# Attention scores of a hybrid decoder layer as split products over 128 rows, with a third weight place for one more unit

## Chip, cores, metric

One NeuronCore of a Trainium2 chip runs the whole layer. The metric is the device time of one execution in microseconds (us), the median over several executions; lower is better. Engines are named as in the profile: PE is TensorE (PEld its weight loads), DVE VectorE, ACT ScalarE, POOL GpSimd, SP SyncE, which here only issues DMAs.

## What is computed

One decoder layer over 512 tokens of width 1024, in float32. One input projection gives the inputs of two token mixers and their gates. Mixer A is a gated linear recurrence (4 heads of 128). Mixer B, which the change touches, scores all causal keys with a small indexer, keeps the 128 best keys of each query, and attends to these with 8 heads of 64 and a T5 relative bias. Cut to what matters:

```python
proj = einsum('bld,dn->bln', x, w_in) + b_in
score = einsum('bth,bths->bts', w, relu(q_idx . k_idx))    # indexer, 8 heads of 64
idx = top_k(where(causal, score, -inf), 128)               # per query, shared by heads
logits = q . k[idx] * 64 ** -0.5 + rel_bias[t5_bucket(qpos - idx)]
ob = softmax(logits) . v[idx]
merged = sigmoid(ga) * ((norm(oa) * silu(za)) @ w_up_a) + sigmoid(gb) * ((ob * silu(zb)) @ w_up_b)
out = layer_norm(ALPHA * x + merged @ w_out)
```

## The kernel before

**Split products.** float32 accuracy of the large projections comes from splitting both operands into a high part in float32r (fp32r, reduced float32) and a low part, the rest. `split_product` (lines 478 to 481) then issues three products: high x high, high x low, low x high. ScalarE makes the high parts of the weights (`split_hi`, line 792), GpSimd or VectorE the low parts (`split_lo`, lines 1570 and 1399).

**Units and quarters.** The weight matrix is cut into units of 256 columns (`UNITS`; the index is the unit's number: 7 is qb0, 8 kb0, 9 and 10 vb, 11 qb1, 12 kb1, 13 and 14 ia, 15 and 16 fa, 17 and 18 qa, 19 to 22 ga). A unit is four quarters of twelve products with 512 columns, and the quarter q is the clock of everything: each engine runs its own hand-written loop over q and calls `side(q)`, which holds the work that is planned beside the projections. On TensorE `side(q)` comes behind quarter q's products, in order; nothing is reordered at run time, and the engines meet at semaphores alone. A unit's first half fills `proj_bank[0]`, its second half `proj_bank[1]`. Each must be emptied (`leave_bank`, line 812 on ScalarE and 1140 on VectorE) before the next unit's same half, two quarters after it was filled. For qb and kb, ScalarE empties it with one activation and the bias (line 859); for vb and ia it is VectorE with an addition (line 1167).

**Weights.** SyncE loads a unit's raw weights, 1 MB in two halves, into one of two raw places by parity; the load of unit u waits for the low parts of unit u-2 (`wait_lo`). High and low parts have three places (`SLOTS`, `slot`): the third is shared in time with x, with gate inputs and with the residual. `hi_quarter(u)` is the quarter in which ScalarE rounds unit u: 4(u-1), or earlier for units in `EARLY_HI`. VectorE makes the low parts of units 17 to 24 (`LO_DVE`), piece 0 in the quarter behind that, pieces 1 to 3 one later (`low_parts`).

**Mixer B.** The indexer's products `dots` (lines 600 and 601) run in quarters 12 to 23, two heads a quarter, as fp32r over 128 rows: the query tile holds a head's high and low part one above the other. VectorE sums them into `score[b]` for query blocks b = 1, 2, 3 with (b+1) x 128 keys. Then `topk_round` (lines 1206 and 1207), 16 rounds per block that each find and strike out 8 keys, following `topk_rounds()`; a last pass makes the penalty tile `pen[b]`. Attention is 32 items (b, head), in pairs, first heads 0 to 3, then 4 to 7; `Q_ITEM` says in which quarter. For an item: `scores` on TensorE (line 611, one fp32 product over the head's 64 rows; the heads of a pair lie in rows 0 to 63 and 64 to 127), GpSimd prepares bias plus penalty in `logit`, `logits` on VectorE subtracts and takes the maximum (line 1230), `softmax_exp` on ScalarE, `invert_sums` on VectorE (line 1241), `normalise` on ScalarE, two quarters later `turn_probs` (transposes, line 620), `move_probs` on VectorE, and `attend` (line 635). The order within VectorE's `side(q)` is: leave bank, index scores, moves, gates, logits, top-k rounds, reciprocals, low parts, mixer A.

**Mixer A.** `tree` holds its products by level (64, 32, ... 1), for p = 0 from quarter 73 and p = 1 from 82 (`Q_TREE`). ScalarE computes the exponentials of each level (`level_factors`) behind VectorE's distances (line 424) and copies results of levels 64 and 32 out of the banks (`tree_copy`, lines 959 and 967); the banks `log_bank` are two, taken in turn.

## Time and profile before

| What | Value |
|---|---|
| median of 3 runs | 469.42 us (469.35 to 471.55) |
| the profiled execution | 468.56 us, of it span 466.8 us |
| TensorE / its weight loads | 456.4 us (98%) / 362.9 us (78%) |
| VectorE, ScalarE, GpSimd busy | 281.4, 217.7, 162.4 us |
| mean granted TensorE clock | 0.995 of 2.4 GHz |
| DMA | 45.64 MB, mean 98 GB/s |

Read it as: the execution's own time holds the span, from its first to its last instruction, and 1.8 us around it. Busy times of engines overlap. TensorE's products are pipelined, so a product's own duration is longer than the step from its start to the next one's; the steps are what adds up.

### The profile page before, as it was taken

How to read it: one execution, taken by the hardware profiler on the slowest of the kernel's cores; microseconds unless marked ns; L12 is line 12 of the kernel's file. 1: busy time of each engine (PE TensorE's matmuls, PEld its weight loads, DVE VectorE, ACT ScalarE, POOL GpSimd, SP SyncE). 2: the span in 40 equal slices, each digit the busy share in tenths (PEclk: the TensorE clock that was granted, in tenths of full speed). 3: DMA queues.
4: the chain of work that ended last, by engine and by line, in shares of the span. 5: the costliest groups of instructions: out<-in, count | busy, mean ns of one | idle time of the engine just before them, and what ended most of it. 6: DMA issues, size and time to landing. Idle time of an engine off the chain costs nothing.

```text
span 466.8 us, 7633 instructions
## 1 busy us (share of the span) xinstructions
PE 456.4 (98%) x2970; PEld 362.9 (78%) x2970; DVE 281.4 (60%) x542; ACT 217.7 (47%) x369; POOL 162.4 (35%) x161
## 2 busy tenths in 40 slices
PE   8999999999999999999999899999999999999993
PEld 6778888888777777777887687787888888888883
DVE  4446589999995333343999984971532332562286
ACT  5635454341327445274876666825872333341000
POOL 0444442492259823481004000000044444994000
PEclk9999999999999999999999999999999999999997
DMA  8818112243022420202021220222033232275022
GB/s 269 268 44 292 57 68 91 90 163 108 0 91 67 134 72 1 91 0 92 18 95 70 91 93 2 93 93 90 0 120 136 87 110 90 94 242 207 0 90 91
DMA packets 15876, 45.64 MB, mean 98 GB/s; under 512 B 2232, under 2 KB 3808, under 8 KB 15840
## 3 DMA queue, kind: packets, MB, share of 16 engines
q1 hardware_dynamic: 15600, 44.96, 28.7%
q8 instruction: 24, 0.39, 0.3%
q10 hardware_dynamic: 240, 0.20, 0.1%
q14 instruction: 12, 0.10, 0.1%
HBM read 43.04 MB, written 2.11 MB: 97 GB/s over the span
## 4 chain that ended last, share of the span: by engine, by line
PE 89%; DVE 6%; issue 2%; ACT 1%; DMA 1%; DVEq 0%; SPq 0%; ACTq 0%
PE bank L479 25%; PE bank L481 24%; PE bank L480 24%; PE bank L611 3%; PE bank L707 2%; PE bank L682 2%; PE bank L635 2%; PE bank L620 2%; DVE w_lo L1399 1%; DMA w_raw<-in_w_units 1%; PE bank L601 1%; PE bank L600 1%; PE bank L525 1%; PE bank L521 1%; PE bank L693 1%
## 5 line engine op out<-in xcount | busy, mean ns | idle before, releaser
L1570 POOL TENSOR_TENSOR w_lo<-w_raw,w_hi 128x512 fp32r<-128x512 f32 x92 | 120.9, 1344 | 166.9 <-ACT w_hi L792 160.2
L479 PE MATMUL bank<-x_hi,w_hi 128*128 128x512 f32 x336 | 134.6, 400 | 0.0
L481 PE MATMUL bank<-x_hi,w_lo 128*128 128x512 f32 x336 | 131.1, 390 | 0.0
L480 PE MATMUL bank<-x_lo,w_hi 128*128 128x512 f32 x336 | 131.0, 390 | 0.0
L479 PEld LDWEIGHTS bank<-x_hi,w_hi 128*128 128x128 f32 x336 | 63.0, 188 | 18.1 <-issue 5.5
L481 PEld LDWEIGHTS bank<-x_hi,w_lo 128*128 128x128 f32 x336 | 63.1, 188 | 13.7
L480 PEld LDWEIGHTS bank<-x_lo,w_hi 128*128 128x128 f32 x336 | 63.2, 188 | 12.0
L792 ACT ACTIVATE w_hi<-w_raw 128x1024 fp32r<-128x1024 f32 (+1 forms) x66 | 66.7, 1028 | 10.9 <-PE bank L481 5.5
L877 ACT ACTIVATE prob<-prob,nmax 128x128 f32<-128x128 f32 (+3 forms) x32 | 17.8, 556 | 47.5 <-DVE nmax L1230 47.4
L1218 DVE COPY prob_t<-bank 128x128 f32<-128x128 f32 (+3 forms) x32 | 14.2, 485 | 31.7 <-PE bank L620 31.6
L1206 DVE MAX8 best<-score 128x8 f32<-128x256 f32 (+2 forms) x48 | 26.8, 558 | 1.0
L1207 DVE MATCH_REPLACE8 score<-best,score 128x256 f32<-128x256 f32 (+2 forms) x48 | 26.0, 542 | 0.0
L479 PE MATMUL bank<-w_hi,x_hi 128*128 128x512 f32 x64 | 25.8, 403 | 0.0
L1399 DVE TENSOR_TENSOR w_lo<-w_raw,w_hi 128x512 fp32r<-128x512 f32 x36 | 23.4, 686 | 3.4 <-ACT w_hi L792 3.4
L481 PE MATMUL bank<-w_hi,x_lo 128*128 128x512 f32 x64 | 25.0, 391 | 0.0
L480 PE MATMUL bank<-w_lo,x_hi 128*128 128x512 f32 x64 | 24.9, 390 | 0.0
L479 PE MATMUL bank<-o_hi,w_hi 128*128 128x512 f32 x64 | 24.9, 389 | 0.0
L480 PE MATMUL bank<-o_lo,w_hi 128*128 128x512 f32 x64 | 24.9, 389 | 0.0
L481 PE MATMUL bank<-o_hi,w_lo 128*128 128x512 f32 x64 | 24.9, 389 | 0.0
L1588 POOL TENSOR_TENSOR logit<-t,pen 128x256 f32<-128x256 f32 x24 | 17.4, 742 | 11.9 <-DVE nmax L1230 11.9
L885 ACT ACTIVATE prob<-prob,prob_rcp 128x128 f32<-128x128 f32 (+3 forms) x32 | 16.3, 556 | 10.3 <-DVE prob_rcp L1241 10.3
L1196 DVE SCALAR_TENSOR_TENSOR score<-relus,w_idx,score 128x256 f32<-128x256 f32 (+2 forms) x21 | 15.8, 751 | 7.8 <-ACT relus L867 6.1
(199 smaller groups left out, 716.6 us busy)
## 6 DMA issues: line engine op xcount, KB each, us to landing
w_raw<-in_w_units SPq DMA_DIRECT2D x66, 512.0 KB, 4.6
out<-y_sb SPq DMA_DIRECT2D x8, 256.0 KB, 2.0
x_raw_hi<-in_x_t SPq DMA_DIRECT2D x4, 256.0 KB, 5.6
w_raw<-in_w_units SPq DMA_DIRECT2D x4, 256.0 KB, 5.9
x_raw_lo<-in_x_t SPq DMA_DIRECT2D x4, 256.0 KB, 6.1
t_turned<-t_row SPq DMA_DIRECT2D x1, 1024.0 KB, 9.7
x_res_hi<-in_x_tok SPq DMA_DIRECT2D x2, 512.0 KB, 5.1
x_res_lo<-in_x_tok SPq DMA_DIRECT2D x2, 512.0 KB, 6.7
```

The source lines that it names most:

```text
L479: nc.tensor.matmul(dst, a_hi, b_hi, start=first, stop=False)
L480: nc.tensor.matmul(dst, a_hi, b_lo, start=False, stop=False)
L481: return nc.tensor.matmul(dst, a_lo, b_hi, start=False, stop=last)
L792: nc.scalar.activation(split_target(u, kiwi_hi, x_hi, w_hi)[:, k, :], raw(u)[:, k, :], ACT.Copy).then_inc(done, 1)
L877: nc.scalar.activation(prob[:, i % 4, 0:n], prob[:, i % 4, 0:n], ACT.Exp, bias=nmax[:, i % 4:i % 4 + 1], scale=-1.0, accum_out=prob_sum[:, ...
L885: nc.scalar.activation(prob[:, i % 4, 0:n], prob[:, i % 4, 0:n], ACT.Copy, scale=prob_rcp[:, i % 4:i % 4 + 1]).then_inc(norm_done, 1)
L1196: ins = nc.vector.scalar_tensor_tensor(out=score[b][:], in0=relus[:, i % 2, 0:n], scalar=w, in1=score[b][:], op0=ALU.mult, op1=ALU.add)
L1206: link(nc.vector.max(best8[:], score[b][:]))
L1207: link(nc.vector.match_replace(score[b][:], best8[:], score[b][:], TAKEN))
L1399: nc.vector.tensor_tensor(split_target(u, kiwi_lo, x_lo, w_lo)[:, k, :], raw(u)[:, k, :], split_target(u, kiwi_hi, x_hi, w_hi)[:, k, :].bi ...
L1570: nc.gpsimd.tensor_tensor(split_target(u, kiwi_lo, x_lo, w_lo)[:, k, :], raw(u)[:, k, :], split_target(u, kiwi_hi, x_hi, w_hi)[:, k, :].bi ...
L1588: nc.gpsimd.tensor_tensor(logit[:, i % 2, n - band:n], t5[:, h, 2 * P - band:], pen[b][:, n - band:] if b else causal_sb[:], ALU.add).then ...
```

## The change

What it does, part by part:

- `scores` issues two fp32r products over 128 rows in place of one fp32 product over 64. For head h, `q_hi(h)` and `q_lo(h)` hold the query's high and low part twice, in rows 0 to 63 and 64 to 127, and `k_hl(h)` holds the key's high part in the head's own rows and its low part in the other rows. So both products with `k_hl(h)` add up to all four part products.
- `leave_bank` for qb and kb: ScalarE rounds each head's 64 rows on its own (two activations a tile instead of one), and VectorE then subtracts to get the low part (two operations a tile, new) and frees the bank. SyncE copies q's rows to the other half (`both_halves`, eight DMAs a group of four heads, behind the loads of units 10 and 14, after a wait for qb0 or qb1), and TensorE's scores wait for these copies.
- The factor 1/8 moves from q and its bias to the logits' scale; the T5 table is multiplied by 8 as it leaves its bank, and `bias_q` is gone.
- The tiles are laid out anew over others that are free by then, with waits for these (`row_out`, `t5_done`, `relu_used`).
- `topk_rounds`: blocks 1, 2 and 3 start at quarters 18, 28, 37 (were 18, 27, 36) at 1.7, 1.7 and 1.5 rounds a quarter (were 1.8). `turn_t5` goes from quarters 31 and 33 to 27 and 29.
- `side` on VectorE: `invert_sums` comes behind the first planned top-k round of the quarter instead of behind all.
- Unit 17 takes the third place; units 17, 18 and 19 are rounded at quarters 61, 65 and 69 (were 64, 68, 72). Low parts follow them, those of unit 19 at quarters 74 and 75 (were 73 and 74). The parity of the places from unit 18 on turns round, and the last two units of `w_out` swap.
- `side` on ScalarE: the copy of level 64 comes ahead of the quarter's `level_factors`.

```diff
@@ -76,8 +76,9 @@
 JOINT = {UNITS.index(n + "0"): UNITS.index(n + "1") for n in ("vb", "ia")}
-EARLY_HI = {9: 30, 10: 32, 13: 46, 14: 48}
-SLOTS = {8: 2, 9: 0, 10: 1, 11: 2, 12: 0, 13: 1, 14: 2}
+EARLY_HI = {9: 30, 10: 32, 13: 46, 14: 48, 17: 61, 18: 65, 19: 69}
+LO_FROM = {19: 73}
+SLOTS = {8: 2, 9: 0, 10: 1, 11: 2, 12: 0, 13: 1, 14: 2, 17: 2}
 Q_DOTS = 4 * 3
@@ -98,7 +99,7 @@
     plan = {}
-    for b, first, per in ((1, 18, 1.8), (2, 27, 1.8), (3, 36, 1.8)):
+    for b, first, per in ((1, 18, 1.7), (2, 28, 1.7), (3, 37, 1.5)):
         for r in range(ROUNDS):
@@ -139,19 +140,25 @@
-            k_hi2, k_lo2 = sb("k_hi2", [P, SEQ], F32R, s), sb("k_lo2", [P, SEQ], F32R, s)
+            with ExitStack() as s2:
+                k_hi2, k_lo2 = (sb(n, [P, SEQ], F32R, s2) for n in ("k_hi2", "k_lo2"))
+            q_lo_01 = sb("q_lo_01", [P, 2, SEQ], F32R, s)
             with ExitStack() as s2:
                 q_hl = sb("q_hl", [P, HEADS_I, SEQ], F32R, s2)
-            q_b, k_b = sb("q_b", [P, 4, SEQ], stack=s), sb("k_b", [P, 4, SEQ], stack=s)
+            q_hi_g1, q_lo_g1 = (sb(n, [P, 4, SEQ], F32R, s) for n in ("q_hi_g1", "q_lo_g1"))
             score = {b: sb(f"score{b}", [P, (b + 1) * P], stack=s) for b in range(1, TB)}
             wi_t = score[TB - 1][64:WKI, :]
-            relus = sb("relus", [P, 2, SEQ], stack=s)
+            with ExitStack() as s2:
+                relus = sb("relus", [P, 2, SEQ], stack=s2)
+            q_lo_23 = sb("q_lo_23", [P, 2, SEQ], F32R, s)
             v_b = sb("v_b", [P, TB, D_B], stack=s)
...
             t5 = sb("t5", [P, HEADS_B, 2 * P], stack=s)
-            t5_turned = sb("t5_turned", [P, HEADS_B, 2 * P], stack=s)
+            with ExitStack() as s2:
+                t5_turned = sb("t5_turned", [P, HEADS_B, 2 * P], stack=s2)
+            k_hl_g0 = sb("k_hl_g0", [P, 4, SEQ], F32R, s)
             pen = {b: sb(f"pen{b}", [P, (b + 1) * P], stack=s) for b in range(1, TB)}
@@ -187,12 +194,16 @@
         with ExitStack() as s:
+            q_hi_g0 = sb("q_hi_g0", [P, 4, SEQ], F32R, s)
+        with ExitStack() as s:
             hot_sb, table = sb("hot_sb", [BUCKETS, T5W], stack=s), sb("table", [HEADS_B, T5W], stack=s)
...
+        with ExitStack() as s:
+            k_hl_g1 = sb("k_hl_g1", [P, 4, SEQ], F32R, s)
         k_c = sb("k_c", [P, 2, 2 * SEQ])
@@ -201,7 +212,6 @@
         bias = sb("bias", [P, 2 * NMAIN])
-        bias_q = sb("bias_q", [P, 2 * NMAIN])
         bias_ia, bias_vb = sb("bias_ia", [P, D_A]), sb("bias_vb", [P, D_B])
@@ -235,7 +245,8 @@
         table_full, table_done = sem("table_full"), sem("table_done")
-        pool_set, bias_q_done = sem("pool_set"), sem("bias_q_done")
+        pool_set, qk_hi_done = sem("pool_set"), sem("qk_hi_done")
+        q_twice = [[sem(f"q_twice{g}_{i}") for i in range(2)] for g in range(2)]
         lb_step, lb_exp, lb_log, dve_step = (sem(n) for n in ("lb_step", "lb_exp", "lb_log", "dve_step"))
@@ -272,7 +283,7 @@
         def slot(u):
-            return SLOTS.get(u, u % 2 if u < 8 else (u + 1) % 2)
+            return SLOTS.get(u, (u + 1) % 2 if 8 < u < 17 else u % 2)
@@ -359,6 +370,17 @@
+        def q_hi(h):
+            return (q_hi_g0, q_hi_g1)[h // 4][:, h % 4, :]
+        def q_lo(h):
+            if h < 4:
+                return (q_lo_01, q_lo_23)[h // 2][:, h % 2, :]
+            return q_lo_g1[:, h % 4, :]
+        def k_hl(h):
+            return (k_hl_g0, k_hl_g1)[h // 4][:, h % 4, :]
         def queries(b):
@@ -432,6 +454,14 @@
                 sp.dma_start(w_raw[:, u % 2, c], w_units[u - 1][:, c]).then_inc(w_in[u % 2][a], 16)
+            def both_halves(g):
+                for i in range(2):
+                    wait_proj_out(sp, f"qb{g}", i)
+                    for h in (4 * g + 2 * i, 4 * g + 2 * i + 1):
+                        for tile in (q_hi(h), q_lo(h)):
+                            sp.dma_start(tile[rows(h + 1), :].bitcast(F32), tile[rows(h), :].bitcast(F32)).then_inc(q_twice[g][i], 16)
@@ -455,6 +485,8 @@
                     sp.dma_start(t5_row, table[:]).then_inc(row_out, 16)
+                if u in (10, 14):
+                    both_halves((10, 14).index(u))
                 if u == 5:
@@ -605,11 +637,12 @@
                 if b == 0 and h % 2 == 0:
-                    wait_proj_out(pe, f"qb{h // 4}", h // 2 % 2)
+                    pe.wait_ge(q_twice[h // 4][h // 2 % 2], 16 * 4)
                     wait_proj_out(pe, f"kb{h // 4}", h // 2 % 2)
                 n = (b + 1) * P
-                nc.tensor.matmul(dst[:, 0:n], q_b[rows(h), h // 2, queries(b)], k_b[rows(h), h // 2, 0:n],
-                                 start=True, stop=True).then_inc(log_full, 1)
+                nc.tensor.matmul(dst[:, 0:n], q_hi(h)[:, queries(b)], k_hl(h)[:, 0:n], start=True, stop=False)
+                nc.tensor.matmul(dst[:, 0:n], q_lo(h)[:, queries(b)], k_hl(h)[:, 0:n],
+                                 start=False, stop=True).then_inc(log_full, 1)
@@ -818,7 +851,7 @@
                 c = 2 * u + i
-                func, b_col, scale = ACT.Identity, bias[:, c:c + 1], 1.0
+                func, b_col = ACT.Identity, bias[:, c:c + 1]
                 if kind == "ki":
@@ -830,11 +863,15 @@
                     return
-                elif kind == "qb":
-                    dst, b_col, scale = q_b[:, tile, :], bias_q[:, c:c + 1], QSCALE
-                    act.wait_ge(bias_q_done, 1)
-                elif kind == "kb":
-                    dst = k_b[:, tile, :]
+                elif kind in ("qb", "kb"):
+                    if name == "qb0" and i == 0:
+                        act.wait_ge(row_out, 16)
+                    if name == "kb0" and i == 0:
+                        act.wait_ge(t5_done, 2)
+                    for h in (2 * tile, 2 * tile + 1):
+                        nc.scalar.activation((q_hi if kind == "qb" else k_hl)(h)[rows(h), :], proj_bank[i][rows(h), :],
+                                             ACT.Identity, bias=bias[rows(h), c:c + 1]).then_inc(qk_hi_done, 1)
+                    return
                 elif kind in ("zb", "za"):
@@ -856,7 +893,7 @@
                         act.wait_ge(mix_done, tile - 3)
-                nc.scalar.activation(dst, proj_bank[i][:], func, bias=b_col, scale=scale).then_inc(proj_out[i], 1)
+                nc.scalar.activation(dst, proj_bank[i][:], func, bias=b_col).then_inc(proj_out[i], 1)
@@ -1028,12 +1065,16 @@
                         near_factors(p)
+                for p, n in tree_at(q):
+                    if TREE[n] == ("lv", 0):
+                        tree_copy(p, n)
                 for p in range(2):
...
                 for p, n in tree_at(q):
-                    tree_copy(p, n)
+                    if TREE[n] != ("lv", 0):
+                        tree_copy(p, n)
                 for p in range(2):
@@ -1159,6 +1200,20 @@
                     ins.then_inc(proj_out[i], 1)
+                elif kind in ("qb", "kb"):
+                    c, tile = 2 * u + i, 2 * int(name[2]) + i
+                    hi_before = 4 * (2 * (tile // 2) + (kind == "kb")) + 2 * i
+                    if name == "qb0" and i == 1:
+                        dve.wait_ge(relu_used, len(DOTS))
+                    for e in range(2):
+                        h = 2 * tile + e
+                        dve.wait_ge(qk_hi_done, hi_before + e + 1)
+                        hi = (q_hi if kind == "qb" else k_hl)(h)[rows(h), :]
+                        lo = q_lo(h)[rows(h), :] if kind == "qb" else k_hl(h)[rows(h + 1), :]
+                        ins = nc.vector.scalar_tensor_tensor(out=lo, in0=proj_bank[i][rows(h), :],
+                                                             scalar=bias[rows(h), c:c + 1], in1=hi.bitcast(F32),
+                                                             op0=ALU.add, op1=ALU.subtract)
+                    ins.then_inc(proj_out[i], 1)
                 elif kind in ("vb", "ia"):
@@ -1228,7 +1283,7 @@
                 nc.vector.tensor_tensor_reduce(out=prob[:, i % 4, 0:n], in0=log_bank[i % 2][:, 0:n],
-                                               in1=logit[:, i % 2, 0:n], scale=-1.0, scalar=3e38,
+                                               in1=logit[:, i % 2, 0:n], scale=-QSCALE, scalar=3e38,
                                                op0=ALU.add, op1=ALU.min,
@@ -1406,10 +1461,10 @@
-            def low_parts(u, j):
-                if u and u + 1 in LO_DVE:
-                    for piece in ((), (0,), (1, 2, 3), ())[j]:
-                        split_lo(u + 1, piece)
+            def low_parts(q):
+                for u in LO_DVE:
+                    for piece in {1: (0,), 2: (1, 2, 3)}.get(q - LO_FROM.get(u, hi_quarter(u)), ()):
+                        split_lo(u, piece)
@@ -1465,12 +1520,15 @@
                     logits(i)
-                for b, r in rounds.get(q, ()):
+                planned = rounds.get(q, [])
+                for b, r in planned[:1]:
                     topk_round(b, r)
...
                     invert_sums(i)
+                for b, r in planned[1:]:
+                    topk_round(b, r)
                 if q < Q_TREE[0]:
-                    low_parts(u, j)
+                    low_parts(q)
                 for p in range(2):
@@ -1490,7 +1548,7 @@
                 if q >= Q_TREE[0]:
-                    low_parts(u, j)
+                    low_parts(q)
                 for p, n in tree_at(q):
@@ -1520,7 +1578,6 @@
             dve.wait_ge(early_in, 32)
-            nc.vector.tensor_scalar(bias_q[:], bias[:], QSCALE, None, ALU.mult).then_inc(bias_q_done, 1)
             for q in range(4 * NMAIN):
@@ -1529,9 +1586,10 @@
                     dve.wait_ge(table_full, 1)
-                    nc.vector.tensor_copy(table[:], turn_bank[0][0:HEADS_B, 0:T5W]).then_inc(table_done, 1)
-                if q in (Q_ITEM[0] - 8, Q_ITEM[0] - 6):
-                    turn_t5(0 if q == Q_ITEM[0] - 8 else 4)
+                    nc.vector.tensor_scalar(table[:], turn_bank[0][0:HEADS_B, 0:T5W], 1 / QSCALE, None,
+                                            ALU.mult).then_inc(table_done, 1)
+                if q in (Q_ITEM[0] - 12, Q_ITEM[0] - 10):
+                    turn_t5(0 if q == Q_ITEM[0] - 12 else 4)
             merge(KT - 1)
@@ -1688,7 +1746,7 @@
             b_cols[:, 2 * u], b_cols[:, 2 * u + 1] = b_in[c:c + P], b_in[c + P:c + UW]
-    for n in range(NOUT):
+    for n in (0, 1, 3, 2):
         units.append(unit(a["w_out"][0][:, n * UW:n * UW + UW]))
```

## Rows read from the trace of the kernel before

**Rows 1.** The page: busy time of each engine, and VectorE's slices

```profile
PE 456.4 (98%) x2970; PEld 362.9 (78%) x2970; DVE 281.4 (60%) x542; ACT 217.7 (47%) x369; POOL 162.4 (35%) x161
...
DVE  4446589999995333343999984971532332562286
```

**Rows 2.** The page: the chain that ended last, by line

```profile
PE bank L479 25%; PE bank L481 24%; PE bank L480 24%; PE bank L611 3%; PE bank L707 2%; PE bank L682 2%; PE bank L635 2%; PE bank L620 2%; DVE w_lo L1399 1%; DMA w_raw<-in_w_units 1%; PE bank L601 1%; PE bank L600 1%; PE bank L525 1%; PE bank L521 1%; PE bank L693 1%
```

**Rows 3.** Groups by shape: line, tiles, shapes xcount | busy us, mean ns | idle

```profile
L611 PE MATMUL bank<-k_b,q_b 64*128 64x512 f32 x16 | 4.5, 641 | 0.0
```

**Rows 4.** TensorE's timeline at three places with scores: start us, us

```profile
120.03 0.49 PE L611 MATMUL bank<-k_b,q_b 64*128 64x128 f32 x4
120.46 0.50 PE L479 MATMUL bank<-w_hi,x_hi 128*128 128x512 f32 x1
...
132.35 0.38 PE L620 MATMUL bank<-id_sb,prob 128*128 128x128 f32 x2
132.66 0.70 PE L611 MATMUL bank<-k_b,q_b 64*128 64x256 f32 x4
133.29 0.50 PE L479 MATMUL bank<-x_hi,w_hi 128*128 128x512 f32 x1
133.63 0.39 PE L480 MATMUL bank<-x_lo,w_hi 128*128 128x512 f32 x1
...
162.50 1.13 PE L611 MATMUL bank<-k_b,q_b 64*128 64x512 f32 x4
163.56 0.50 PE L479 MATMUL bank<-w_hi,x_hi 128*128 128x512 f32 x1
```

**Rows 5.** The same at a place with transposes and no scores

```profile
191.85 0.38 PE L620 MATMUL bank<-id_sb,prob 128*128 128x128 f32 x2
191.99 0.47 PE L479 MATMUL bank<-w_hi,x_hi 128*128 128x512 f32 x1
192.30 0.39 PE L480 MATMUL bank<-w_lo,x_hi 128*128 128x512 f32 x1
```

**Rows 6.** The same at two places with the indexer's dots

```profile
47.55 0.28 PE L600 MATMUL bank<-k_hi,q_hl 128*128 128x256 f32 x1
...
48.02 0.40 PE L479 MATMUL bank<-x_hi,w_hi 128*128 128x512 f32 x1
...
75.52 0.39 PE L600 MATMUL bank<-k_hi,q_hl 128*128 128x512 f32 x1
...
76.42 0.39 PE L479 MATMUL bank<-x_hi,w_hi 128*128 128x512 f32 x1
76.65 0.39 PE L480 MATMUL bank<-x_lo,w_hi 128*128 128x512 f32 x1
```

**Rows 7.** VectorE: its timeline in quarter 38, and the group of line 1158

```profile
117.77 0.69 DVE L1167 TENSOR_TENSOR v_b<-bank,bias_vb 128x512 f32<-128x512 f32 x1
118.37 0.69 DVE L1206 MAX8 best<-score 128x8 f32<-128x512 f32 x1
...
119.88 0.69 DVE L1206 MAX8 best<-score 128x8 f32<-128x512 f32 x1
...
L1158 DVE SCALAR_TENSOR_TENSOR q_hl<-bank,bias,q_hl 64x512 fp32r<-64x512 f32 x8 | 6.0, 748 | 12.3 <-ACT q_hl L830 12.3
```

**Rows 8.** The timelines of VectorE, TensorE and ScalarE around the first tree

```profile
241.03 1.89 DVE L1399 TENSOR_TENSOR w_lo<-w_raw,w_hi 128x512 fp32r<-128x512 f32 x3
...
252.23 0.69 PE L682 MATMUL bank<-q_r,k_l 128*64 128x64 f32 x16 [0.31 <-DVE k_l L1291]
...
255.40 0.63 ACT L938 ACTIVATE dec<-dec 128x512 f32<-128x512 f32 x1 [2.87 <-DVE dec L424]
...
257.26 0.73 PE L682 MATMUL bank<-q_c,k_c 128*32 128x16 f32 x64 [0.72 <-ACT att L959]
...
266.17 0.27 PE L682 MATMUL bank<-q_c,k_c 128*32 128x16 f32 x10 [0.93 <-issue]
```

**Rows 9.** The page, DMA issues: count, KB each, us to landing

```profile
w_raw<-in_w_units SPq DMA_DIRECT2D x66, 512.0 KB, 4.6
```

## Prediction

> **What bounds the kernel now.** The page comes first. TensorE is busy 456.4 of 466.8 us, VectorE 281.4, ScalarE 217.7 [rows 1], and the chain that ended last is TensorE for most of its length, nearly three quarters of the span in the three products of the large projections (lines 479 to 481) [rows 2]. So a microsecond counts only if TensorE issues less, switches less or waits less. The slices say where TensorE could lose time to a partner: VectorE stands at 9 tenths in slices 7 to 12, 70 to 140 us, where the top-k rounds are [rows 1]. After that I read TensorE's timeline around the attention scores, which the change rewrites, then VectorE's in the full stretch, then both around the first tree.
>
> A quarter is twelve products of the projections; what the plan gives TensorE beside it stands behind it. Sixteen of these places hold a pair of score items.
>
> **Part 1, scores: columns.** Today an item is one fp32 product over 64 rows, recorded as two passes; the two heads of a pair lie in different halves of the rows. For 512 keys the four passes run from 162.50 to 163.56, 1.06 us; for 256 keys 0.63, for 128 keys 0.43 [rows 4]. That is 0.21 for each further 128 keys, so 384 keys stand at 0.85. One pass alone has 641 ns [rows 3], so four in 1.06 us means that they overlap two by two. After the change a pair is four fp32r products over 128 rows. The trace has that form in the indexer's dots: four of 512 keys take 0.90 us (75.52 to 76.42), four of 256 take 0.47 (47.55 to 48.02) [rows 6], and the middle, 0.69, is my estimate for 384. There are four pairs of each length. Gain: 4 x (0.16 + 0.16 + 0.16) = 1.9 us for 256, 384 and 512 keys.
>
> The Trainium skill, "TensorE: Matmul & The Clock Gate", section on packing small matmuls, speaks against this part: products whose operands lie in different row groups run in the array at once, and a product over all 128 rows gives that up. The trace agrees that the passes overlap [rows 3, 4]. If an fp32 pass ran at the fp32r column rate, the overlap would make today's pairs half as long as the new ones, and the part would lose about 5 us instead of gaining 1.9; the sum would be some 471. The row decides, since the overlapping passes take 0.53 us for 512 columns and an fp32r product 0.23.
>
> For 128 keys no fp32r row exists. Between ends: at the 256-key cadence halved, four take 0.24, a gain of 4 x 0.19 = 0.8 us over the kernel; at the worst, each takes what an unoverlapped fp32 pass of 128 keys takes, half of 0.43, so 0.86 for four and a loss of 1.7. I take the row whose weight load has the same 128 columns: transposes of 128 columns, two in 0.14 to 0.31 with the switch in it [rows 4, 5], about 0.11 each, so 0.44 for four. Gain 0.
>
> **Part 2, scores: switches.** The first projection product behind an fp32 score starts its successor late: 133.29 to 133.63 is 0.34 us, where the usual step is 0.23 (76.42 to 76.65) [rows 4, 6]. Compare a place with transposes alone and one with transposes and scores: 191.85 to 192.30 is 0.45, 132.35 to 133.63 is 1.28 [rows 4, 5]. The difference, 0.83, is the pair's own 0.63 and 0.20 more, one switch beyond that of the transposes. The dots show no such step on either side [rows 6]. As the new scores have the projections' format, I take 0.20 away at 15 of the 16 places (at the sixteenth the scores follow the value products directly, and a switch stays). 15 x 0.20 = 3.0 us. Ends: 0, if the step belongs to something else, and 3.2.
>
> **Part 3, the work that the new operands cost.** Each of the eight q/k tiles leaves its bank by two ScalarE activations instead of one, and by two new VectorE subtractions of 64x512 at 0.75 us [rows 7]: 12 us on VectorE at most, 16 x 0.67 = 10.7 if they follow one another at the step of the neighbouring form (the v_b addition starts 0.60 before its successor). Half of it, qb0 and kb0, falls in quarters 30 to 36, where VectorE has no idle time. ScalarE is at half load and its eight extra activations I cost at nothing; their cover is the two quarters that a bank has until TensorE wants it again.
>
> VectorE reaches the v_b tile of quarter 38 at 117.77 [rows 7]. In the new plan it has 5.4 to 6.0 us more before that, and two rounds of 1.51 us (118.37 to 119.88) fewer, since block 3 starts a quarter later and slower. So it gets there at 120.2 to 120.8 and is through at 120.8 to 121.4. TensorE wants that bank at 120.46 [rows 4], 0.2 earlier once scores are cheaper. That is a new wait of 0.5 to 1.1 us; I take 0.7. Queued behind it on TensorE is everything; on VectorE the logits of items 0 and 1. At quarter 40 the same sum (0.60 v_b, 1.51, 0.43 logits, 3.03 for two rounds) leaves VectorE at about 126.5, and TensorE wants the bank at 126.8 plus the wait it has had: no second wait. The rounds then last to quarter 47 instead of 44, in front of the penalty of block 3, which is first needed for the item of quarter 51. Ends: 0, and 4 us if it lags throughout.
>
> The reciprocal goes behind one round, which brings the normalised probabilities 1.5 us earlier. Transposes two quarters on were just in time, so this gains nothing; it keeps part 3 from costing another wait.
>
> The lower row halves of q travel on SyncE's queue, four copies of 128 KB per tile pair, sixteen in all. SyncE now waits for qb0 before it issues the load of unit 11, about 4 us later than today. A load of 512 KB lands in 4.6 us [rows 9] and unit 11 is rounded only at quarter 40, past 120 us; the first scores wait for copies that left near 104. Hidden; without that cover a copy's landing of some 5 us would show. T5's turning moves four quarters forward on VectorE, same work. The dropped bias scaling and the table's scaling are one small operation each, nothing.
>
> **Part 4, first tree.** TensorE waits 0.72 us at 257.26 for ScalarE's copy of level 64, and that copy stood behind exponentials that waited 2.87 us for VectorE's distances; at 252.23 it waits 0.31 for VectorE's k_l [rows 8]. With the copy first, it can run at about 253, and the wait goes. With a third place for unit 17, its low parts and those of units 18 and 19 move: three of 0.60 us at 241.03 [rows 8] leave the stretch ahead of k_l. So k_l comes 1.8 us earlier, and the 0.31 goes too. Next late would be the level products, which gain as much. Gain 1.0 us. The stall of 0.93 at 266.17 names no partner ("issue") [rows 8]; I leave it in. Ends of part 4: 0 and 2. The swap of the last two output units follows from the slots and costs nothing: same loads, same order of size.
>
> **Sum.** Against the profiled execution, 468.56 us: -1.9 (columns) + 0 (128 keys) - 3.0 (switches) + 0.7 (new wait) - 1.0 (tree) = -5.2, so 463.4. The median of the runs, 469.42, is 0.86 above that execution: 464.3.
>
> **Rivals.** A: fp32r at 128 columns is as slow as its upper bound. For: no row shows it. Against: 256 columns show no such thing. 464.3 + 1.7 = 466.0; chance 0.2. B: the switch step isn't one of format but comes with a group of products over other tiles. For: a step stands behind transposes too, 191.99 to 192.30 [rows 5]. Against: the dots have none. 464.3 + 3.0 = 467.3; 0.1. C: VectorE lags from quarter 38 to 47, with TensorE waiting at several banks and transposes, 4 us in all instead of 0.7: 467.6; 0.14. For: slices at 9. D, slower: the banks. Every q/k bank is now freed by VectorE, behind whatever round it is in. TensorE wants it two quarters after the part is done, 24 x 0.227 = 5.4 us; if VectorE comes more than about 4 us after the part, each of eight releases shows a round and its two subtractions, 1.5 us: 12 us instead of 0.7, so 475.6. For: a saturated engine in a path that ScalarE had free. Against: in quarter 38 VectorE comes at 117.77 to a part that TensorE ended at 114.5 or so (two quarters before 120.0), 3.2 us, with fewer rounds ahead of it from now on in each quarter. Chance 0.06. My forecast keeps 0.5.
>
> The Trainium skill, "FP8 and Floating Point Precision", on the data path, says that true fp32 passes the array four times. By it, overlap counted, columns would gain nothing, and the sum would be 466.2; the rows show two passes of 0.53 us.
>
> **Numbers.** Half a per cent, 2.35 us, is what a measurement can tell from no change: the border is 467.1. The forecast, A, and a part of B and C lie below it: 0.78. Within: most of B and C, 0.15. Slower: D, 0.07. Low end: 464.3 - 0.8 (128 keys) - 0.7 (no new wait) - 1.0 (the issue stall gone) = 461.8. High end 468.0 takes in C.
>
> **What would show it.** Score products as 128*128 of 128x512, twice 64, four in 0.90 us; the product behind them 0.23 us before its successor; a wait of TensorE for VectorE's v_b near 120 us, 0.5 to 1.1 us; no wait for the level-64 copy. Wrong would be: several waits of TensorE for q, k or v banks, fp32r products of 128 columns above 0.2 us each, or 0.34 us steps that stay.

## The result and the profile after

| us | before | after |
|---|---|---|
| median of 4 runs each | 469.58 (469.35 to 471.55) | 464.56 (464.45 to 464.77) |
| profiled execution (span) | 468.56 (466.8) | 464.45 (462.6) |

The ratio is 0.9885, with a 95% interval of 0.9858 to 0.9912. Between the medians lie 5.0 us, between the two profiled executions 4.1. The profiled execution of before was 0.9 to 1.0 below its median, that of after 0.1 below. Everything that follows explains the 4.1; which waits the other runs of before had more of, no profile shows.

The page after, the lines that answer to [rows 1] and [rows 2]:

```profile
PE 451.7 (98%) x2970; PEld 367.2 (79%) x2970; DVE 290.7 (63%) x557; ACT 223.2 (48%) x377; POOL 161.5 (35%) x161
...
DVE  4446589999999563346989975952523241562286
...
PE bank L511 24%; PE bank L512 23%; PE bank L513 23%; DVE score L1262 3%; DVE best L1261 3%; PE bank L668 2%; PE bank L740 2%; PE bank L715 2%; PE bank L653 2%; DMA w_raw<-in_w_units 1%; PE bank L633 1%; PE bank L632 1%; PE bank L643 1%; PE bank L644 1%; PE bank L553 1%
```

TensorE is 4.7 us less busy, VectorE 9.3 more, and the top-k rounds (lines 1261 and 1262, 1206 and 1207 before) now stand in the chain with 6%. The projections' products are lines 511 to 513 now. The four longest of TensorE's own waits after (line, partner, us in total, times, longest):

```profile
PE bank L511 <- DVE w_lo L1454: 1.2, 1, 1.2
PE bank L784 <- POOL eps L1619: 1.1, 1, 1.1
PE bank L511 <- DVE q_lo_g L1213: 0.6, 1, 0.6
PE bank L511 <- DVE v_b L1222: 0.6, 1, 0.6
```

The first, third and fourth are new; only the fourth was forecast.

**Scores.** TensorE's timeline after, at three pairs: 128 keys in quarter 40, 128 keys in a place with nothing else, and 512 keys behind transposes (start us, us, then the operation and in brackets the idle time before it):

```profile
119.89 0.22 PE L643 MATMUL bank<-k_hl_g,q_hi_g 128*128 128x128 f32 x1
...
121.04 0.50 PE L511 MATMUL bank<-w_hi,x_hi 128*128 128x512 f32 x1 [0.60 <-DVE v_b L1222]
...
181.33 0.39 PE L513 MATMUL bank<-w_hi,x_lo 128*128 128x512 f32 x1
181.55 0.22 PE L643 MATMUL bank<-k_hl_g,q_hi_g 128*128 128x128 f32 x1
181.61 0.28 PE L644 MATMUL bank<-k_hl_g,q_lo_g 128*128 128x128 f32 x1
181.72 0.27 PE L643 MATMUL bank<-k_hl_g,q_hi_g 128*128 128x128 f32 x1
181.84 0.27 PE L644 MATMUL bank<-k_hl_g,q_lo_g 128*128 128x128 f32 x1
181.95 0.45 PE L511 MATMUL bank<-w_hi,x_hi 128*128 128x512 f32 x1
182.23 0.40 PE L512 MATMUL bank<-w_lo,x_hi 128*128 128x512 f32 x1
...
170.99 0.48 PE L643 MATMUL bank<-k_hl_g,q_hi_g 128*128 128x512 f32 x1
...
171.53 0.40 PE L643 MATMUL bank<-k_hl_g,q_hi_g 128*128 128x512 f32 x1
171.77 0.39 PE L644 MATMUL bank<-k_hl_g,q_lo 128*128 128x512 f32 x1
172.00 0.40 PE L511 MATMUL bank<-w_hi,x_hi 128*128 128x512 f32 x1
```

A short product's record overlaps its neighbour's, so a place is best priced by starts: from the start of the last projection product ahead of it to the start of the second behind it, less the two steps of 0.227 us that would be there anyway. At 181.33 that is 0.90 - 0.45 = 0.45 us for four products of 128 keys; their steps are 0.11 each. The same place before cost 0.62. For 512 keys the steps are 0.23. A single step can mislead, as a record can start early: at the transposes of [rows 5] the product behind them starts 0.14 us after the first of two and has a step of 0.31 behind it. From 191.85 to 192.30 less the product's own 0.23 leaves 0.22 for two transposes, 0.11 each, so nothing is lost there.

The table prices every place that differs, after less before:

| Where | after - before, us |
|---|---|
| 16 score places: 128 keys 4 x -0.17; 256 keys 4 x -0.35; 384 keys 4 x -0.34; 512 keys 3 x -0.33 and -0.11 | -4.5 |
| wait for v_b, 121.04 (0.65 in the place, 0.17 of it hidden by the cheaper scores) | +0.8 |
| wait for q's bank, 155.98 | +0.9 |
| three waits in the first tree | -1.4 |
| wait for w_lo, 256.37, and the step behind it | +1.5 |
| the stall before the level product, 266.17 before | -1.1 |
| the rest, no entry over 0.12 | -0.3 |
| sum, entries rounded | -4.2 |

The start of the very last projection product went from 459.36 to 455.15, 4.2 earlier.

### The profile page after: what moved, and what is told of

Same layout as the page of the kernel before. It is cut to its first block, busy times and chain, and to the rows that moved or that the text cites. A ratio compares the mean times of both kernels' runs of the same rounds, so it can differ in the third digit from the quotient of the medians.

```text
span 462.6 us, 7676 instructions
## 1 busy us (share of the span) xinstructions
PE 451.7 (98%) x2970; PEld 367.2 (79%) x2970; DVE 290.7 (63%) x557; ACT 223.2 (48%) x377; POOL 161.5 (35%) x161
## 4 chain that ended last, share of the span: by engine, by line
PE 86%; DVE 10%; issue 1%; DMA 1%; ACT 1%; DVEq 0%; SPq 0%; ACTq 0%
PE bank L511 24%; PE bank L512 23%; PE bank L513 23%; DVE score L1262 3%; DVE best L1261 3%; PE bank L668 2%; PE bank L740 2%; PE bank L715 2%; PE bank L653 2%; DMA w_raw<-in_w_units 1%; PE bank L633 1%; PE bank L632 1%; PE bank L643 1%; PE bank L644 1%; PE bank L553 1%
## 5 line engine op out<-in xcount | busy, mean ns | idle before, releaser
L1488 DVE TENSOR_TENSOR mix<-bank,gate_a_hi 128x512 f32<-128x512 f32 x4 | 2.8, 692 | 29.4 <-PE bank L513 29.4
L904 ACT ACTIVATE relus<-bank 128x256 f32<-128x256 f32 (+2 forms) x24 | 10.5, 490 | 21.3 <-PE bank L633 21.3
```

What stands on the lines that cost most here:

```text
L904: nc.scalar.activation(relus[:, i % 2, 0:n], log_bank[i % 2][:, 0:n], ACT.Relu, scale=QSCALE).then_inc(log_out[i % 2], 1)
```

## The experiments

All are edits of the changed kernel except the one that says otherwise. Compared are profiled executions by the same account of places; the medians stand beside them where there are any; the runs for which one time is given were executed once. The changed kernel's own profiled execution is 464.45.

### What an fp32 pass costs: one product over 128 rows

```diff
-matmul(dst[:, 0:n], q_hi(h)[:, queries(b)], k_hl(h)[:, 0:n], start=True, stop=False)
-matmul(dst[:, 0:n], q_lo(h)[:, queries(b)], k_hl(h)[:, 0:n], start=False, stop=True)
+matmul(dst[:, 0:n], q_hi(h)[:, queries(b)].bitcast(F32), k_hl(h)[:, 0:n].bitcast(F32), start=True, stop=True)
```

> The changed kernel with each score as one fp32 product over the same 128 rows of the same tiles (the product with the query's low part is left out, and the tiles are read as fp32). My theory: the step of 0.20 us at a place with scores is one of format, and the 64-row passes of two heads overlapped in the kernel before. Then a pair of 512 keys takes four unoverlapped passes of 0.53 us, 2.1 us (1.7, 1.3 and 0.84 for 384, 256 and 128 keys), the first projection product behind it starts its successor after 0.34 us again, and the kernel takes 464.6 + 13.7 + 2.9, some 479 to 482 us. Rival B (the step comes with any group over other tiles, and not with the format): no 0.34 us step behind the scores, since tiles and rows are those of the changed kernel. Rival to the overlap (two heads only share a pass's time): a pair of 512 keys stays at 1.06 us and the kernel at about 468.

Measured: 470.87 us, between the two expectations and outside both. TensorE's timeline at the pair of 512 keys, then at the pair of 128 keys with nothing else:

```profile
173.24 1.88 PE L643 MATMUL bank<-k_hl_g,q_hi_g 128*128 128x512 f32 x4
174.56 0.79 PE L511 MATMUL bank<-w_hi,x_hi 128*128 128x512 f32 x1
175.19 0.39 PE L512 MATMUL bank<-w_lo,x_hi 128*128 128x512 f32 x1
...
184.26 0.39 PE L513 MATMUL bank<-w_hi,x_lo 128*128 128x512 f32 x1
184.49 0.60 PE L643 MATMUL bank<-k_hl_g,q_hi_g 128*128 128x128 f32 x4
...
185.16 0.40 PE L512 MATMUL bank<-w_lo,x_hi 128*128 128x512 f32 x1
```

From 173.24 to 175.19 less the projection product's own 0.23 is 1.72 us for four passes, 0.43 each. Before, four passes over 64 rows took 1.06 [rows 4]: they do overlap, by a factor of 1.6, not 2. At 128 keys four passes over 64 rows took 0.43 [rows 4], no less than four of 0.11 here, so there they did not gain by it. The 641 ns that one pass has as its record [rows 3] is not the rate at which passes follow each other. At 128 keys this kernel costs what the changed one costs, 0.11 a step; at 256, 384 and 512 keys it costs 0.39, 0.58 and 0.80 more, four times each, 7.1 in all, and 1.0 comes back because two waits for VectorE shrink. And no switch step appears, though the format is fp32: from 184.26 to 185.16 is 0.90 us, as in the changed kernel from 181.33 to 182.23, where the kernel before took 0.17 more. So format does not make the step.

The prediction weighed the Trainium skill, "FP8 and Floating Point Precision", on four passes for true fp32. Two recorded passes of 0.43 are 0.86 us for an item of 512 keys; four at the fp32r step of 0.227 would be 0.91. Here the trace agrees with the page better than with the prediction's reading, "two passes of 0.53". The new scores gain columns all the same because the overlap saves less than half: 1.06 for the old pair against 0.90 for the new.

### What the step belongs to: fp32r over 64 rows

```diff
-matmul(..., q_hi(h)[:, queries(b)], k_hl(h)[:, 0:n], start=True, stop=False)
-matmul(..., q_lo(h)[:, queries(b)], k_hl(h)[:, 0:n], start=False, stop=True)
+matmul(..., q_hi(h)[rows(h), queries(b)], k_hl(h)[rows(h), 0:n], start=True, stop=True)
```

> The changed kernel with each score as one fp32r product of high part by high part over the head's 64 rows (the three other part products are left out). The run with fp32 over 128 rows had no step of 0.34 us behind its scores, so format is not what makes it. New theory: the step comes with products that use part of the array's rows or columns. Then it is back here although the format is the projections' own: the first projection product behind the scores starts its successor after 0.33 to 0.34 us, and TensorE's first score starts 0.31 to 0.32 us behind the last projection product where nothing stands between, against 0.23 in the changed kernel. Theory of my prediction (format): 0.23 at both. If 64-row fp32r products of two heads overlap as the fp32 ones did, a pair of 512 keys takes about 0.25 us, otherwise 0.45.

Measured: 463.97 us. TensorE's timeline at the place that is shown above at 181.33, and at the pair of 512 keys:

```profile
181.44 0.39 PE L513 MATMUL bank<-w_hi,x_lo 128*128 128x512 f32 x1
181.76 0.33 PE L643 MATMUL bank<-k_hl_g,q_hi_g 64*128 64x128 f32 x2
182.02 0.50 PE L511 MATMUL bank<-w_hi,x_hi 128*128 128x512 f32 x1
182.35 0.39 PE L512 MATMUL bank<-w_lo,x_hi 128*128 128x512 f32 x1
...
171.56 0.49 PE L643 MATMUL bank<-k_hl_g,q_hi_g 64*128 64x512 f32 x2
171.99 0.50 PE L511 MATMUL bank<-w_hi,x_hi 128*128 128x512 f32 x1
```

The step is back: 0.32 into the scores and 0.33 out of them, against 0.227, so 0.20 us for both sides. The place as a whole says the same: 0.91 us from 181.44 to 182.35 with two products, where the changed kernel takes 0.90 with four. Format is the projections', rows are 64. With the run before, all four cases are there: fp32 over 64 rows (the kernel before) and fp32r over 64 (here) have the step, fp32 over 128 and fp32r over 128 (the changed kernel) have none. The step goes with products that use part of the rows, whatever their format. The same 0.32 to 0.35 stands on both sides of the level products, 128 rows by 32 columns (after: 257.64 to 257.96, and 258.62 to 258.96). The Trainium skill, "TensorEngine Tiling (Array Packing)", Key Properties, says that a change of tiling mode, not of tile alone, drains TensorE; these two runs agree, at about 0.1 us a change. The transposes, 128 by 128, agree too: their place has no step in it, as worked out above.

The expectation had asked whether fp32r products of two heads overlap as the fp32 passes did: a pair of 512 keys in 0.25 us if so, in 0.45 if not. Both start together, and the next product starts 0.42 later, so they hardly do. Products over 64 rows are therefore no cheaper way to the same accuracy: the high part by the high part alone takes 0.42, and three such pairs, an estimate from that, 1.3 against 0.90 for all four part products in the changed kernel.

### How much of a shorter score arrives: the low-part product left out

```diff
-matmul(..., q_hi(h)[:, queries(b)], k_hl(h)[:, 0:n], start=True, stop=False)
-matmul(..., q_lo(h)[:, queries(b)], k_hl(h)[:, 0:n], start=False, stop=True)
+matmul(..., q_hi(h)[:, queries(b)], k_hl(h)[:, 0:n], start=True, stop=True)
```

> The changed kernel with the product of the query's low part left out, so one fp32r product an item. If score columns are on the path that sets the end, it gains half of what the pairs take, 4 x (0.22 + 0.24 + 0.35 + 0.45) = 5.0 us, less what TensorE then waits longer for VectorE in the top-k stretch (up to quarter 47; at most 1.5 us): 459.5 to 461. If scores were hidden behind VectorE, it stays within 1 us of 464.6. For 128 keys a pair should take 0.22 us, two steps of 0.11, if the weight load sets that step.

Measured: 462.05 us, 2.4 less than the changed kernel: less than the 3.6 to 5.1 that the expectation gives to scores on the path, more than the 1 of its rival. Of the missing part 0.7 is the opening, which began later (23.31 for 22.62) with nothing edited there. Places away from waits fall by 0.22 to 0.47 us, as priced. But TensorE now comes to the banks earlier than VectorE; its list of waits has

```profile
PE bank L511 <- DVE q_lo_g L1212: 1.8, 2, 1.3
...
PE bank L511 <- DVE v_b L1221: 0.8, 1, 0.8
```

The changed kernel has 0.6 and 0.6. From quarter 40 to quarter 50 the places change by -0.23, -0.24, -0.24, +0.39 and +0.31, nothing in sum. So between quarters 40 and 50 VectorE, not TensorE, sets the time.

### Rounds and reciprocal on VectorE: four variants

All rounds ahead of the reciprocal, as before the change:

```diff
-for b, r in planned[:1]:
+for b, r in planned:
     topk_round(b, r)
 ...
-for b, r in planned[1:]:
-    topk_round(b, r)
```

> The changed kernel with the reciprocals behind all top-k rounds of their quarter again. My theory: the new order covers what the new subtractions cost VectorE. Without it ScalarE's normalisation comes 1.5 us later in quarters 39, 41, 43 and 45 and the transposes two quarters on wait: by the changed kernel's times the normalised pair is ready at about 126.7 for a transpose at 126.6, so waits of 0 to 0.5 us at three or four transposes: 464.6 + 0.3 to 1.5 us. Rival (the order is worth nothing): within 0.2 us and no wait of TensorE for ScalarE's prob.

Measured: 467.07 us. Of the 2.6 more, 1.1 lies in the opening (the first projection product starts at 23.75 instead of 22.62), where nothing was edited, and 1.5 in waits: +0.94 in quarter 48, +0.39 in quarter 50, +0.11. They are waits for q's banks, not for transposes:

```profile
PE bank L511 <- DVE q_lo_g L1213: 1.7, 2, 1.0
```

Why the reciprocal decides about a bank is seen around the wait of 155.98 in the changed kernel, on VectorE, ScalarE and TensorE:

```profile
151.01 0.67 DVE L1262 MATCH_REPLACE8 score<-best,score 128x512 f32<-128x512 f32 x1
151.72 0.72 DVE L1264 TENSOR_SCALAR pen<-score 128x512 f32<-128x512 f32 x1
152.36 0.15 DVE L1296 RECIPROCAL prob_rcp<-prob_sum 128x2 f32<-128x2 f32 x1
154.41 1.51 DVE L1213 SCALAR_TENSOR_TENSOR q_lo_g<-bank,bias,q_hi_g 64x512 fp32r<-64x512 f32 x2 [1.90 <-ACT q_hi_g L872]
```

```profile
152.54 1.12 ACT L922 ACTIVATE prob<-prob,prob_rcp 128x384 f32<-128x384 f32 x2 [1.39 <-DVE prob_rcp L1296]
153.69 1.40 ACT L872 ACTIVATE q_hi_g<-bank,bias 64x512 fp32r<-64x512 f32 x2
```

```profile
155.98 0.50 PE L511 MATMUL bank<-x_hi,w_hi 128*128 128x512 f32 x1 [0.63 <-DVE q_lo_g L1213]
```

Round, penalty and reciprocal on VectorE; ScalarE waits 1.39 for the reciprocal, normalises, and only then rounds the high parts; VectorE waits 1.90 for these, subtracts for 1.51, and TensorE waits 0.63 for that. Though both engines idle in turn, the path is closed: VectorE, ScalarE, VectorE, TensorE. From quarter 47 on the reciprocal can come ahead of all rounds:

```diff
-for b, r in planned[:1]:
+for b, r in planned[:q < 47]:
     topk_round(b, r)
 ...
-for b, r in planned[1:]:
+for b, r in planned[q < 47:]:
     topk_round(b, r)
```

> The changed kernel with the reciprocal ahead of the last top-k round in quarter 47 (there the round and the penalty pass, 2.2 us, stood ahead of it; ScalarE came to the tile of qb1 only behind its normalisation). Theory: the wait of TensorE at quarter 50 for q's low part (0.6 us shown, 0.9 by start times) is this chain, DVE reciprocal, ScalarE normalisation, ScalarE rounding of q, VectorE subtraction. Then it goes or shrinks below 0.2: 464.6 - 0.8 = 463.8. Rival (VectorE's backlog itself is late): the wait stays within 0.2 us of what it is.

Measured: 463.68 us (463.38 to 463.88), ratio 0.9878 (0.9863 to 0.9892). The wait for q's bank is gone from the list, -0.87 at its place.

Block 3 a quarter later:

```diff
-for b, first, per in ((1, 18, 1.7), (2, 28, 1.7), (3, 37, 1.5)):
+for b, first, per in ((1, 18, 1.7), (2, 28, 1.7), (3, 38, 1.6)):
```

> The changed kernel with block 3's rounds from quarter 38 at 1.6 a quarter instead of from 37 at 1.5; both end in quarter 47. Theory: the wait of TensorE for v_b at quarter 40 (0.6 us shown, 0.8 by start times) is only the two rounds that stand ahead of v_b's addition, 3.0 us. Then it goes, and nothing else does: 464.6 - 0.8 = 463.8. Rival (VectorE is overfull up to quarter 47 and the wait only moves): a wait of similar length at quarters 42 to 48, time within 0.3 us.

Measured: 466.36 us, ratio 0.9937 (0.992 to 0.9954). The wait for v_b is gone (-0.82), and 2.7 come back, 0.47 in quarter 48 and 2.23 in quarter 50:

```profile
PE bank L653 <- ACT prob L922: 1.6, 1, 1.6
PE bank L511 <- DVE q_lo_g L1213: 1.2, 2, 1.0
```

Only one round of block 3 put behind v_b:

```diff
-plan.setdefault(first + int(r / per), []).append((b, r))
+plan.setdefault(first + int(r / per) + ((b, r) == (3, 1)), []).append((b, r))
```

> The changed kernel with one round of block 3 moved from quarter 37 to 38, behind v_b's addition; all later rounds stand as they are. The start at 38 for all of block 3 took the wait for v_b away (0.82 us by start times) but left VectorE one round and a half behind at quarters 46 to 49 and cost 2.7 us there. Theory: with the later plan unchanged the wait goes and no other comes: 464.6 - 0.8 = 463.8. Rival (TensorE is then ahead of VectorE by what it gained, and the wait comes back at quarter 42 or 48): within 0.3 us of 464.6.

Measured: 464.87 us, ratio 0.9898 (0.9867 to 0.9929). The v_b wait is gone (-0.82), and +0.35, +0.17 and +0.32 stand in quarters 42, 48 and 50. So the v_b wait is not a price of that place: VectorE has so much work from quarter 38 to 50, and moving a round moves the wait. The reciprocal gained because it shortened a path, not VectorE's queue.

### The first tree

Part 4 alone, on the kernel before (the copy ahead, the third place, `LO_FROM`, the quarters of rounding, the order of the last units):

```diff
-EARLY_HI = {9: 30, 10: 32, 13: 46, 14: 48}
+EARLY_HI = {9: 30, 10: 32, 13: 46, 14: 48, 17: 61, 18: 65, 19: 69}
+LO_FROM = {19: 73}
...
+for p, n in tree_at(q):
+    if TREE[n] == ("lv", 0):
+        tree_copy(p, n)
```

> The kernel before with the fourth part alone (third place for unit 17, units 17 to 19 rounded earlier, low parts of unit 19 a quarter later, level 64 copied first, the last two output units swapped); scores and top-k as before. By the two traces: the waits at quarters 74, 75 and 76 go (0.38 + 0.91 + 0.10) and a wait for the low parts of unit 19 comes (1.2), so 469.5 - 0.2, no change that can be measured, unless the stall of 1.1 us at quarter 77 (code that arrives late behind a load of weights) goes too, since that load is released a quarter later: then 468.2. Rival (the part is worth the 1.0 us of my prediction): 468.5 with no wait for low parts.

Measured: 468.27 us, ratio 0.9976 (0.9967 to 0.9986), its profiled execution 468.66. The same entries as in the table: -0.38, -0.91 and -0.09 in the tree, +1.46 for w_lo, -1.12 for the stall, and 0.4 more around quarter 72. The median is 1.2 us below that of the kernel before measured beside it (469.43), which is what was expected if the stall goes; the profiled execution began its projections 0.6 later and shows less. Part 4 by itself gains 1 to 3 thousandths.

The copy behind the exponentials again, the places kept:

```diff
-for p, n in tree_at(q):
-    if TREE[n] == ("lv", 0):
-        tree_copy(p, n)
 ...
-    if TREE[n] != ("lv", 0):
-        tree_copy(p, n)
+    tree_copy(p, n)
```

> The changed kernel with level 64 copied behind the exponentials again. My theory: the copy's place removed TensorE's wait at quarter 75. Then that wait is back, 0.5 to 0.9 us, named ScalarE att, but VectorE's low parts of unit 19 come at the same time as now, so the wait for them at quarter 76 (1.18 us) shrinks by the same amount: 464.6 to 465.0. Rival (the earlier low parts alone removed it, as VectorE's distances come 4 us earlier): no wait for att, no change in time.

Measured: 465.14 us; the 0.7 more lies in the opening, which ran 0.8 later with nothing edited there. No wait for the copy came back, against the theory: it runs at 251.79 instead of 249.52 and is still early. So moving the copy is worth nothing once k_l comes early, and the low parts moved out of VectorE's stretch ahead of k_l carry the gain. What the copy's move would give in the kernel before, without them, was not run.

The changed kernel around the tree, in turn VectorE, ScalarE and TensorE, which answers to [rows 8]:

```profile
246.03 1.22 DVE L1346 TENSOR_TENSOR k_l<-k_l,k_a 128x1024 f32<-128x1024 f32 x1
...
255.64 1.89 DVE L1454 TENSOR_TENSOR w_lo<-w_raw,w_hi 128x512 fp32r<-128x512 f32 x3
```

```profile
249.52 0.77 ACT L996 ACTIVATE att<-bank 64x256 f32<-64x256 f32 x2 [2.26 <-PE bank L715]
```

```profile
256.37 0.51 PE L511 MATMUL bank<-x_hi,w_hi 128*128 128x512 f32 x1 [1.18 <-DVE w_lo L1454]
...
261.58 0.74 PE L715 MATMUL bank<-q_c,k_c 128*32 128x16 f32 x64
```

Unit 19's low parts 1 to 3 stand at quarter 75, behind the distances of the tree, and quarter 76 wants them. A quarter earlier:

```diff
-LO_FROM = {19: 73}
+LO_FROM = {19: 72}
```

> The changed kernel with the low parts of unit 19 at quarters 73 and 74, as in the kernel before, instead of 74 and 75. The changed kernel's TensorE waits 1.18 us at quarter 76 for them. My theory: the one quarter's delay is all of that wait. Then it goes and no other takes its place, since VectorE is at k_l 4 us earlier than before: 464.6 - 1.2 = 463.4. Rival (VectorE's work in front of the tree is what counts, wherever the low parts stand): the wait moves to the products of levels 32 and 16 in quarter 75, and the time stays within 0.4 us.

Measured: 464.68 us (464.0 to 464.77; the profiled execution is the 464.0), ratio 0.9896 (0.9882 to 0.9911): no gain that shows in the median. The wait is gone (-1.48), but in a group of 64 level products TensorE's timeline has the stall of before again, +0.86 at its place:

```profile
260.27 0.65 PE L715 MATMUL bank<-q_c,k_c 128*32 128x16 f32 x54
261.59 0.27 PE L715 MATMUL bank<-q_c,k_c 128*32 128x16 f32 x10 [0.67 <-issue]
```

The last 10 of 64 wait for nothing that has a name, the same 10 as in [rows 8]. What differs is the load of unit 21, which these low parts release. The queue of instruction fetches shows one packet of 0.02 MB near each such place. In DMA views of half a microsecond, of before from 263.7 to 264.2 and of after from 257.4 to 257.9, these are the queues:

```profile
q1 hardware_dynamic: 37, 0.12, 58.5%
q8 instruction: 1, 0.02, 11.0%
```

```profile
q8 instruction: 1, 0.02, 11.8%
```

Before, the fetch comes at 263.85, while the load (issued 259.66) fills the engines and 0.7 us ahead of the group of 64, and TensorE stalls; after, it comes as the load is issued (257.55), ahead of its packets and 4.0 us ahead of the group, and TensorE does not. In this run it comes at 259.16, inside a load issued at 254.93 and 1.1 us ahead. So: the earlier low parts, and the load of unit 21 held back until TensorE is through this group of level products.

```diff
-LO_FROM = {19: 73}
+LO_FROM = {19: 72}
...
+if u == 21:
+    wait_lvl_multiplied(sp, 0, 4)
```

> The changed kernel with the low parts of unit 19 a quarter earlier and SyncE's load of unit 21 held until the level-4 products of quarter 77. With the low parts alone TensorE's wait for them went (1.35 us by start times) but a stall of 0.86 us in the level-4 products took its place, with TensorE's code fetched at 259.16, inside the load of unit 21 (issued 254.93, landed 260.01); in the kernel before, fetch 263.85 inside a load from 259.66 to 264.75, stall 1.12. In the changed kernel the fetch started with the load and there was no stall. Theory: code fetched behind a load of weights comes late. Then holding the load removes the stall: 464.6 - 1.3 = 463.2, no wait in quarters 76 and 77. Rival (the stall belongs to the code's place, not to the load): it stays at 0.7 to 1.1 us, 464.6.

Measured: 463.53 us (463.36 to 463.69), ratio 0.9868 (0.9843 to 0.9894); the profiled execution is 1.1 below the changed kernel's. Wait and stall are both gone. TensorE's timeline, and the DMA view from 256.8 to 261.2, in which the fetch is the only transfer:

```profile
260.38 0.74 PE L717 MATMUL bank<-q_c,k_c 128*32 128x16 f32 x64
```

```profile
q8 instruction: 1, 0.02, 1.4%
```

The stall is shown to hang on the load: only the load's time differs between this run and the one ahead of it. That the code packet is what is late is argued, since no run moved the packet alone. For it: in the two kernels with the stall the packet starts 0.7 and 1.1 us ahead of the group of 64, in the ten others with the same number of products on TensorE (2970) 2.9 to 4.1. But a fetch late and inside a load is not enough for a stall. In the runs with the low-part product left out and with 64 rows it starts at 258.47 and 260.74, inside loads issued at 255.11 and 257.03, 0.7 and 0.3 us ahead of the group, and TensorE does not stand. These two have 32 products fewer (2938), so the same packet may hold code of a later place; no run shows that.

### Both together

The edits of the last run and of the reciprocal at quarter 47.

> The changed kernel with the two edits that gained, in one: the reciprocal ahead of the last round in quarter 47 (463.68 alone) and the low parts of unit 19 a quarter earlier with the load of unit 21 held (463.53 alone); the round behind v_b, which gained nothing, is left out. The waits they remove lie at quarters 50 and 76, far apart, so the gains should add: 464.6 - 0.9 - 1.0 = 462.7, with one named wait of TensorE left between quarter 12 and the end, that for v_b at quarter 40. If the earlier TensorE meets VectorE's tree work sooner (rival), part comes back as a wait in quarters 74 to 77 and the time is 463.2 to 463.5.

Measured: 462.62 us (462.58 to 462.72), ratio to the kernel before 0.9856 (0.984 to 0.9873). It beats both kernels: its slowest run lies 1.7 below the fastest of the changed kernel. The gains add as expected. TensorE's waits:

```profile
PE bank L786 <- POOL eps L1621: 1.1, 1, 1.1
PE bank L555 <- ACT w_hi L827: 0.6, 1, 0.6
PE bank L513 <- DVE v_b L1224: 0.6, 1, 0.6
```

## Why the prediction was right, and where it was lucky

The forecast of 464.3 against 464.56 measured is closer than its terms. Against its own base, the profiled execution, it said -5.2, and -4.1 came. The forecast then added 0.86, by which that execution lay below its median, and after the change the profiled execution lies only 0.1 below: that is luck, and it hides most of the miss of 1.1.

- **Columns, -1.9, and 128 keys, 0: right.** Four products of 128 keys take 0.45 (0.44 predicted), of 512 keys 0.9. The row that was chosen, weight loads of 128 columns, was the right neighbour. The Trainium skill, "TensorE: Matmul & The Clock Gate", on LDWEIGHTS, gives a weight load the number of its columns divided by 1.2 in ns, so by estimate 107 ns for 128 columns; the steps of 0.11 agree. Rival A falls.
- **Switches, -3.0: right in amount, wrong in reason.** Columns and switches together gave -4.5 for -4.9, and the sixteenth place, where a switch was said to stay, gave 0.11 where the others of its length gave 0.33. The step is not one of format but of how many rows or columns of the array are in use, and the 0.20 is both its sides. The prediction took it for one switch beyond that of the transposes, but these have none, and so the sign for rival B, the step of 0.31 behind them, falls. Its cause, a group over other tiles, falls too: the new scores have no step. The reason matters: fp32 products over 128 rows would have saved the step, fp32r over 64 would not.
- **The wait for v_b, +0.7: right.** VectorE began v_b at 120.30, predicted 120.2 to 120.8; the wait cost 0.8.
- **"No second wait": the step that failed.** The prediction followed VectorE to quarter 40 and stopped. In quarter 50 q's bank was 0.9 late: the last round and the penalty of quarter 47 end on VectorE only at 152.4, the reciprocal stands behind them, and a q bank is freed by ScalarE and VectorE one after the other. That ScalarE's part costs "nothing" within the two quarters held for each engine alone, not for the two in a row behind a reciprocal. This was rival C's place, with a quarter of its price, and rival D's kind of wait at one release of eight.
- **Reciprocal, 0: right in kind, without a size.** The prediction said that it gains nothing and keeps part 3 from another wait, of transposes, and gave no price. Undone, it costs 1.5, and what waits is a bank.
- **Tree, -1.0: -1.4 came.** k_l starts at 246.03 instead of 250.87, and TensorE is 3.1 earlier there, so k_l comes 1.8 earlier against TensorE, as predicted. That the copy's move gives a part of the gain falls: in the changed kernel it gives none.
- **Low parts of unit 19, costed at nothing: +1.5, the largest miss.** The prediction moved low parts out of the stretch ahead of k_l and never asked where those of unit 19 land. The diff says it: quarters 74 and 75, for use in 76.
- **The stall of 0.93, "I leave it in": it went, -1.1.** It hung on where a load falls, and part 4 moves that load. The low end of the range had it.
- **Copies of q, wait on SyncE's queue, T5, scalings: 0, right.** The page after has copies of q at 3.8 us each from issue to landing, SyncE issued the last of each group at 104.54 and at 157.74, and TensorE's list of waits has none for them.

So +0.9, +1.5 and 0.4 of the scores' gain were missed on one side, and -1.1, -0.4 and the rest of -0.3 on the other; errors of both signs cancelled to within 1.1 us.

## What to carry to other kernels

Price a place by starts, from the last product ahead to the second behind; it takes in entry and exit steps and needs no trust in modelled ends, nor in the single start record behind a change of work. When a change moves deferrable work, follow every moved piece to its reader, and when a bank needs two engines to empty it, add up their path with what is queued ahead of each; on a saturated engine moving one piece shifts a wait, and only cutting a path between engines removes it. A reason can be wrong where its number is right, so change one property at a time (rows, then format) before using it elsewhere.

## What had not been expected of the hardware

- A change between products over all rows and columns and products over part of them costs about 0.1 us on each side (0.32 and 0.33 for a step of 0.227), in fp32r as in fp32; fp32 over 128 rows has none, and transposes of 128 by 128 have none.
- An fp32 pass of 512 columns takes 0.43 us alone, and two over different halves of the rows 0.53 together. Two fp32r products of 512 columns over different halves take 0.42 together, against 0.23 for one over all rows. At 128 columns an fp32 pass and an fp32r product both take 0.11.
- TensorE stood 0.7 and 0.9 us ahead of the last 10 of the same 64 small products in two kernels in which the fetch of a code page began inside a 1 MB load, 0.7 and 1.1 us ahead of these products. Holding the load back took the stall away. Two kernels with 32 products fewer had such a fetch and no stall.
